# Multiplying x by D on ACT in four activations instead of once on GpSimd, with ACT's squares one slot later

## The reference

```python
xf  = xs                                    # (512, 32 heads, 64)
xc  = xf * dt                               # per head and token
cb  = einsum('bclgn,bcsgn->bclsg', cc, bc)  # per chunk of 128 tokens, per group
y_diag = einsum('bclsgj,bcsgjp->bclgjp', cb * decay, xc)
y_off  = einsum('bclgn,bcgjpn->bclgjp', cc, prev) * exp(a_cs)
y = y_diag + y_off + xf * d_skip            # d_skip: one number per head  <- this product moves
y = y * silu(z)
y = y * rsqrt(mean(y * y) + EPS) * ssd_norm_w     # mean over each group's 512 features
ssd_out = y @ w_ssd_o
```

## Time and profile before

| | |
|---|---|
| median of 3 runs | 1032.49 us |
| the profiled execution: its own time | 1032.07 us |
| its span | 1030.3 us |
| PE busy | 1022.4 us (99% of the span) |
| DVE busy | 644.9 us (63%) |
| ACT busy | 466.6 us (45%) |
| POOL busy | 93.4 us (9%) |
| chain that ended last | PE 88%, DVE 9% |
| granted TensorE clock | 0.9 or more of full speed in every slice |

### The profile page before, as it was taken

One profiled execution on the slowest core, in us unless ns is written; L12 is line 12 of the kernel. 1 busy time (PEld: TensorE's weight loads), 2 busy tenths in 40 slices (PEclk: granted clock), 3 DMA queues, 4 the chain that ended last, 5 costly groups with the idle time before them and its releaser, 6 DMA issues.

```text
span 1030.3 us, 13250 instructions
## 1 busy us (share of the span) xinstructions
PE 1022.4 (99%) x4999; PEld 833.9 (81%) x4999; DVE 644.9 (63%) x897; ACT 466.6 (45%) x834; POOL 93.4 (9%) x128
## 2 busy tenths in 40 slices
PE   9999999999999999999999999999999999999997
PEld 8887777777888888888888888898888888888886
DVE  7638998784476686885754544566766676641332
ACT  6335556454545636765633222444444444331233
POOL 0001111110222120122220100000000000000000
PEclk9999999999999999999999999999999999999999
DMA  7622212224646424445362743223232223232222
GB/s 218 123 85 82 82 52 72 83 82 114 164 113 174 130 85 127 141 123 155 102 212 82 253 156 104 81 82 105 99 120 83 81 84 120 88 130 89 94 71 82
DMA packets 123499, 116.49 MB, mean 113 GB/s; under 512 B 21342, under 2 KB 111782, under 8 KB 123447
## 3 DMA queue, kind: packets, MB, share of 16 engines
q1 hardware_dynamic: 95509, 94.74, 29.9%
q10 hardware_dynamic: 25346, 12.59, 5.3%
q0 software_dynamic: 2592, 8.46, 2.2%
HBM read 109.41 MB, written 6.36 MB: 112 GB/s over the span
## 4 chain that ended last, share of the span: by engine, by line
PE 88%; DVE 9%; ACT 1%; issue 1%; POOL 0%; DVEq 0%; ACTq 0%; POOLq 0%
PE banks L1269 27%; PE banks L1271 26%; PE banks L1270 26%; DVE conv_acc L1217 3%; DVE w_lo L870 2%; PE banks L1366 1%; PE banks L1359 1%; PE banks L1354 1%; PE banks L1314 1%; PE banks L1334 1%; ACT probs L621 1%; PE banks L1342 1%; DVE small L948 1%; DVE scores L945 1%; DVE probs L962 0%
## 5 line engine op out<-in xcount | busy, mean ns | idle before, releaser
L870 DVE TENSOR_TENSOR w_lo<-w_raw,w_hi 128x1024 fp32r<-128x1024 f32 (+1 forms) x166 | 200.1, 1245 | 124.1 <-ACT w_hi L583 122.9
L583 ACT ACTIVATE w_hi<-w_raw 128x1024 fp32r<-128x1024 f32 (+1 forms) x166 | 164.1, 1037 | 108.9 <-PE banks L1271 107.6
L1269 PE MATMUL banks<-xn_hi,w_hi 128*128 128x512 f32 x528 | 212.2, 402 | 0.2 <-DVE sz L1229 0.2
L1270 PE MATMUL banks<-xn_lo,w_hi 128*128 128x512 f32 x528 | 206.2, 391 | 0.0
L1271 PE MATMUL banks<-xn_hi,w_lo 128*128 128x512 f32 x528 | 206.1, 390 | 0.0
L1269 PE MATMUL banks<-hn_hi,w_hi 128*128 128x512 f32 (+1 forms) x376 | 141.3, 376 | 0.0
L1270 PE MATMUL banks<-hn_lo,w_hi 128*128 128x512 f32 (+1 forms) x376 | 141.2, 375 | 0.0
L1271 PE MATMUL banks<-hn_hi,w_lo 128*128 128x512 f32 (+1 forms) x376 | 141.2, 375 | 0.0
L1269 PEld LDWEIGHTS banks<-xn_hi,w_hi 128*128 128x128 f32 x528 | 99.2, 188 | 30.5 <-issue 10.4
L1271 PEld LDWEIGHTS banks<-xn_hi,w_lo 128*128 128x128 f32 x528 | 99.1, 188 | 21.6
L1270 PEld LDWEIGHTS banks<-xn_lo,w_hi 128*128 128x128 f32 x528 | 99.3, 188 | 18.8
(11 more groups left out here) (220 smaller groups left out, 1467.5 us busy)
## 6 DMA issues: line engine op xcount, KB each, us to landing
w_raw<-in_w_in SPq DMA_DIRECT2D x29, 1024.0 KB, 5.4
w_raw<-in_w_up SPq DMA_DIRECT2D x22, 1024.0 KB, 5.0
decay<-acs_scratch ACTq DMA_DIRECT2D x16, 512.0 KB, 6.3
w_raw<-in_w_ssd_o SPq DMA_DIRECT2D x8, 1024.0 KB, 5.2
w_raw<-in_w_down SPq DMA_DIRECT2D x8, 1024.0 KB, 5.1
w_raw<-in_w_in SPq DMA_DIRECT2D x16, 256.0 KB, 4.5
w_raw<-in_w_attn_o SPq DMA_DIRECT2D x16, 256.0 KB, 4.9
decay_off<-acs_scratch ACTq DMA_DIRECT2D x32, 128.0 KB, 3.6
```

The source lines that it names most:

```text
L583: A.activation(whi[:, c % 2, lo_:hi_], raw[:, c % 2, lo_:hi_], ACT.Copy).then_inc(w_rounded, 1)
L870: V.tensor_tensor(wlo[:, c % 2, lo_:hi_], raw[:, c % 2, lo_:hi_], f32(whi[:, c % 2, lo_:hi_]), ALU.subtract).then_inc(w_split, 1)
L1269: T.matmul(out_, w[0], m[0], start=first, stop=False)
L1270: T.matmul(out_, w[0], m[1], start=False, stop=False)
```

## The change

Two entries of the table and the place of one operation. `x_skip_term` leaves POOL and goes to ACT at offset 2, one slot behind `bc_out` of the same step; there it is four activations of 128x128 with the column of D as their scale, and the last one signals `d_dxs`, for which DVE's L1016 and L1026 wait. `squares` goes from offset 7 to 8 in ACT's slots.

```diff
@@ SSD_STAGES
-    ("ACT", "squares", 7), ("ACT", "clamp_0", -3), ...
+    ("ACT", "squares", 8), ("ACT", "x_skip_term", 2), ("ACT", "clamp_0", -3), ...
-    ("POOL", "x_skip_term", 1), ("POOL", "sum_tiles", 1))
+    ("POOL", "sum_tiles", 1))
@@ gpsimd
-                        elif what == "x_skip_term":
-                            g, cc = n // NT, n % NT
-                            eng.wait_ge(d_x, n + 1)
-                            eng.wait_ge(pcols, 11)
-                            v_ = xs[:, TG * g:TG * g + TG, cc * P:(cc + 1) * P]
-                            eng.tensor_tensor(v_, v_, dsk[:, TG * g:TG * g + TG].unsqueeze(2)
-                                              .broadcast_to([P, TG, P]), ALU.mult).then_inc(d_dxs, 1)
@@ scalar, rides
+                    elif what == "x_skip_term":
+                        g, cc = n // NT, n % NT
+                        eng.wait_ge(d_x, n + 1)
+                        for t in range(TG * g, TG * g + TG):
+                            v_ = xs[:, t, cc * P:(cc + 1) * P]
+                            ins = A.activation(v_, v_, ACT.Identity, scale=dsk[:, t:t + 1])
+                        ins.then_inc(d_dxs, 1)
```

More of the change, by code:

```diff
@@ L113 @@
     ("ACT", "load_start_decay", 4), ("ACT", "bc_out", 1), ("ACT", "start_decay", 5),
-    ("ACT", "squares", 7), ("ACT", "clamp_0", -3), ("ACT", "clamp_1", -2), ("ACT", "decay", -1), ("DVE", "x_dt", 2),
+    ("ACT", "squares", 8), ("ACT", "x_skip_term", 2), ("ACT", "clamp_0", -3), ("ACT", "clamp_1", -2), ("ACT", "decay", -1), ("DVE", "x_dt", 2),
     ("DVE", "decayed_cb", 3), ("DVE", "new_state", 5), ("DVE", "gated_y", 5), ("POOL", "mask_cb", 0),
-    ("POOL", "x_skip_term", 1), ("POOL", "sum_tiles", 1))
+    ("POOL", "sum_tiles", 1))
 RIDES = {}
```

## The result

The changed kernel takes **1037.32 us** (median of 6 executions, 1035.36 to 1037.69), the kernel before on the same chip 1032.65 us (6 executions, 1032.08 to 1033.22). The ratio is 1.0042, with a 95% interval of 1.0032 to 1.0052: 4.3 us slower, between 3.3 and 5.4. The forecast was 1035.5 us, 3.0 us over its median, in a range up to 1037.2; by the ratio, the change makes 1036.8 us of the 1032.49 us given before it, inside the range and 1.3 us above the forecast (the median as measured lies 0.1 us above the range).

The account below looks back on a forecast made before the run. PE was taken to bound the kernel (88% of the chain of waits). Place one +1.7 and place two +1.3 make 3.0 us; 1032.07 becomes 1035.1, and with 0.42 for the median 1035.5 us, range 1033.0 to 1037.2.

Parts of the forecast that it names:

- Place one: Steps 8 and 9 of the kernel: PE waits for DVE's late L993; +1.7 us remains, 1.0 without turns.
- steps 1 and 2: In kernel step 8, four new ACT activations make DVE 1.17 us late; the squares end 4.0 us later, at 432.97.
- Steps 3 and 4: In kernel step 9, POOL's sums and DVE's L1222 and L918 take turns; mask at 435.45, L993 starts at 435.48.
- Step 5: In kernel step 9, PE wants L993 at 434.55 and gets it at about 436.75: 2.2 us, or 1.5 without turns.
- Step 10's 0.49 us given back: PE's earlier 0.49 us wait for L988 disappears because PE comes later, leaving +1.7 of the 2.2 us.
- Place two: After step 15: squares stand behind `y_hi`, POOL's second sum comes late and PE waits at L1374: +1.3 us.
- Everything else at zero: Other steps, such as 7 and 12 to 14: moved squares stay hidden under PE's margins, costing zero.
- only place two bites: Rival, 15%: DVE isn't late in step 8, PE waits 0.3 us, swallowed at step 10; total +1.3, 1033.8 us.
- relief: Rival, 10%: POOL no longer slows DVE, PE's 0.49 us wait goes, squares come in time; 1032.0 us, not slower.
- third stall: Rival, 12%: in step 11 the mask is late as in step 9, another 1.5 us; 1037.0 us.

Follow-up runs that it names:

- e2: Kernel before with only the squares moved to offset 8, the product staying on POOL: 1035.25 us, ratio 1.0027.
- e3: Changed kernel with the squares of step 15 alone put back at slot 7: 1033.82 us, ratio 1.0016.
- e4: Changed kernel with two dummy matmuls in PE's wait of step 9: 1035.23 us, ratio 1.0029.
- e6: Changed kernel with dummy matmuls in both PE waits, two in step 9 and one before L1374 of step 15: 1035.38 us, ratio 1.0027.
- e1: Changed kernel with the squares back at slot 7, so only the product moves to ACT: 1033.66 us, ratio 1.0010.
- e10: Kernel before with the squares of step 8 alone one slot later, the product left on POOL: 1034.85 us, ratio 1.0022.
- e8: Kernel before with the squares of step 15 alone at slot 8, the product left on POOL: 1034.26 us, ratio 1.0019.
- e12: Kernel before with the squares of step 15 alone at slot 8 and one dummy matmul ahead of L1374: 1033.56 us, ratio 1.0012.
- e9: Kernel before with POOL's product done on one column of each tile instead of 128: 1032.23 us, ratio 0.9997.
- e11: Changed kernel with squares at slot 7 and the product left on POOL in steps 8, 9 and 10: 1031.95 us, ratio 0.9996.

## Why the prediction was right, and what it lacked

- **Place one, steps 1 and 2** (DVE 1.17 us late, squares 4.0 us later): measured 1.17 us, and the squares end at 433.76 − 0.91 = 432.85 against 432.97 in the text.
- **Steps 3 and 4** (the sums and DVE take turns): L918 1.21 us, POOL's sum 1.11 us. L993 starts at 435.35 after the start's offset is taken off, against 435.48.
- **Step 5** (PE waits 2.2 us): L1366 is 437.54 − 434.55 − 0.91 = 2.08 us late. The stretch A alone grew by 1.87; the other 0.2 us came in at L1354, where the forecast had nothing: DVE's L988, late as well, ended at 433.77, and PE started at 433.83. It costs nothing by itself, since the wait for L993 follows, but by my own list it was a place put at zero that showed a small wait.
- **Step 10's 0.49 us given back**: right, −0.49 to −0.54 in e2, e3, e4 and e6, which have the changed order of the squares and no fall of the clock behind step 9. My reason was half of it. I took DVE's idle 1.04 us as a cushion; e1 and e10 show that it is one only because the squares of step 9 move behind L786.
- **Place two, +1.3 us**: C grew by 1.20 and 1.24 in the two profiles of the changed kernel, and by 1.5 in e8. The path was the one foreseen: `y_hi` starts at 531.39 and POOL's sums end at 533.87, 4.06 and 4.09 us later than the text has them, by which PE was late by then (its last matmul ahead of L1374 began at 532.42 instead of 528.44, 3.98 us later).
- **Everything else at zero**: no other new wait of PE in the list from step 0 on, and C is that of before when step 15 is put back.
- **The term that was missing** is in the sum of step 5 and place two: I priced a wait of PE at its length. In part of the executions TensorE's clock falls behind the wait, and that adds about 1.55 us behind step 9 (B 14.45 instead of 12.9) or about as much behind L1374 (e4). The changed kernel has two such waits, so its executions spread over 3.0 us, where the 33 of the kernel before in the last comparison spread over 1.7. The sum 1.87 + 0.2 − 0.5 + 1.2 = 2.8 us holds without a fall (e6: 2.95; the six executions under 1036.5 have a median of 1035.5, my forecast); with one fall it is 4.3, the measured ratio. That the result lies inside the range by its ratio is partly luck: the range was drawn without this term, and the median itself, 1037.32, lies above its end of 1037.2, as four of the six executions do.

Of the rivals, *only place two bites* and *relief* are refuted by A, and a *third stall* would have shown at step 11 and did not. That the clock fell behind PE's waits stands in the traces. That PE's standing idle is what brings it down is made likely, not proved, by the dummies: 0 of 7 executions of e6 above 1036.5 against 6 of 12 of the changed kernel, and 0 of 11 of e12 in an upper group against 5 of 11 of e8, the latter on different chips. What stays open is why it falls in some executions and not in others with the same wait: e2 and e10 wait 1.78 us at L1366 and had no fall in their profiles nor a clear upper group in 8 and 11 executions, while the changed kernel, with 1.70 us, fell there in both profiles. The work around the wait doesn't decide alone: e3 has the same wait amid the same work, and its profile shows none. I have not tested whether the chip or the moment of the launch decides.

## What to carry to other kernels

An operation taken off an engine that nobody waits for bought nothing here (e9), and moving it cost nothing measurable in thirteen of the sixteen steps (e11): only the few places where the bound engine comes shortly after its input decide, so look there first, and leave just those steps as they were. An idle time is a cushion only if its releaser doesn't itself depend on the late engine. And where the bound engine is TensorE, price a wait like those here (1.1 to 1.8 us) once at its length, and once with the fall of the clock behind it (about 1.6 us more); if the wait can't be avoided, try a dummy matmul in it, which went with the loss of the second part here.

## What the runs showed that I had not expected

- A wait of 1.7 us in a stretch where PE was otherwise busy nearly without a break was followed by 3.4 us at 1.2 GHz, with matmuls of 128x512 at 0.42 us apart instead of 0.23; behind a wait of 1.23 us (e4) they came at 0.42 us too. The same wait of 1.7 us in e3 was not followed by it. It shows in no list of waits, only in the column of the granted clock and in the distances.
- With one dummy 128x512 matmul in a wait of 1.4 us there was no upper group of executions (5 of 11 without it, 0 of 11 with it, on another chip).
- POOL's product beside DVE's L993 stretched it from 1.22 to 2.04 us (e2) without making PE wait noticeably longer (1.78 against 1.70 us), since the mask came earlier there (at 434.18, against 436.23 − 0.91 = 435.32 in the changed kernel).
